# Attention steps in another order, angle tables in pieces, and one step instead of two per panel in the first units

## The reference, cut to what matters

```
scores = jnp.einsum("bcqhd,bckhd->bchqk", qc, k_band).astype(jnp.float32) / math.sqrt(d)
scores = jnp.where(valid, scores + bias[None, None], NEG_INF)
probs = jax.nn.softmax(scores, axis=-1).astype(v.dtype)
out = jnp.einsum("bchqk,bckhd->bcqhd", probs, v_band)            # units 0 to 3
...
w = (p1 - lam * p2).astype(vt.dtype)
return jnp.einsum("bhqk,bhkd->bhqd", w, vt)                      # units 4 to 7
...
ang = positions.astype(jnp.float32)[..., None] * inv_freq
return jnp.cos(ang)[:, :, None, :], jnp.sin(ang)[:, :, None, :]
```

## Time and profile before

| | us |
|---|---|
| median of 3 runs | 1624.08 (1623.08 to 1628.35) |
| the profiled execution | 1629.7 |
| its span, first to last instruction | 1627.8 |
| PE busy | 1523.2 (94%) |
| DVE busy | 845.3 (52%) |
| ACT busy | 617.6 (38%) |
| POOL busy | 179.6 (11%) |

### The profile page before, as it was taken

How to read it: one execution, slowest core, us unless ns; L and a number is a source line. 1 busy time by engine, 2 the same in 40 slices (tenths; PEclk the granted TensorE clock), 3 DMA queues, 4 the chain that set the end, 5 groups by cost and what they waited for, 6 DMA issues and landing times.

```text
span 1627.8 us, 18609 instructions
## 1 busy us (share of the span) xinstructions
PE 1523.2 (94%) x7194; PEld 1207.5 (74%) x7194; DVE 845.3 (52%) x1441; ACT 617.6 (38%) x1117; POOL 179.6 (11%) x121
## 2 busy tenths in 40 slices
PE   7988999999899999999889879998999999999996
PEld 5766667788688888888667669666677788888885
DVE  4544455434753444434656876335445665565454
ACT  4544346422452323323445522215334443343233
POOL 0001100001200000000222251000001121121012
PEclk9999999999899999999898979799999999999998
DMA  6221111232323233323321100001123233233221
GB/s 228 78 72 65 53 54 64 78 91 78 104 78 103 92 102 93 100 95 91 110 91 54 63 1 20 27 27 39 53 98 97 78 104 117 91 101 95 91 76 53
DMA packets 39687, 130.22 MB, mean 80 GB/s; under 512 B 4656, under 2 KB 5040, under 8 KB 39600
## 3 DMA queue, kind: packets, MB, share of 16 engines
q1 hardware_dynamic: 39600, 129.03, 24.9%
HBM read 124.82 MB, written 4.19 MB: 79 GB/s over the span
## 4 chain that ended last, share of the span: by engine, by line
PE 81%; DVE 8%; ACT 6%; issue 3%; POOL 1%; DMA 1%; DVEq 0%; SPq 0%; ACTq 0%; POOLq 0%
PE bank L1022 79%; DVE Fm L1662 3%; ACT Fm L1333 3%; PE bank L1025 2%; ACT Whi L1333 2%; DVE Fm L1654 1%; DVE Fm L1749 1%; DVE Wlo L1654 1%; POOL Fm L2205 1%; ACT L1333 0%; DMA Wraw<-in_w_in_dram 0%; DVE sm L1658 0%; DVE Fm L1658 0%; DMA Fm<-in_relb_dram 0%; DVE sm L1662 0%
## 5 line engine op out<-in xcount | busy, mean ns | idle before, releaser
L1022 PE MATMUL bank<-Rm,Whi 128*128 128x512 f32 x2816 | 885.5, 396 | 0.0
L1022 PEld LDWEIGHTS bank<-Rm,Whi 128*128 128x128 f32 x2816 | 541.0, 192 | 112.5 <-issue 0.8
L1022 PE MATMUL bank<-Rm,Wlo 128*128 128x512 f32 x1408 | 572.1, 406 | 21.8 <-DVE Rm L1654 11.3
L1654 DVE TENSOR_TENSOR Wlo<-Wraw,Whi 128x1024 fp32r<-128x1024 f32 (+1 forms) x211 | 258.7, 1228 | 179.2 <-ACT Whi L1333 178.8
L1022 PEld LDWEIGHTS bank<-Rm,Wlo 128*128 128x128 f32 x1408 | 270.7, 192 | 103.3 <-issue 47.1
L1333 ACT ACTIVATE Whi<-Wraw 128x1024 fp32r<-128x1024 f32 (+1 forms) x224 | 232.6, 1042 | 218.8 <-PE bank L1022 210.6
L2205 POOL TENSOR_TENSOR Fm<-Fm 128x512 f32<-128x512 f32 x94 | 142.8, 1527 | 920.1 <-ACT Fm L1333 371.6
L1022 PE MATMUL bank<-Xr,Whi 128*128 128x512 f32 x736 | 226.6, 389 | 0.0
L1333 ACT ACTIVATE Fm<-bank 128x512 f32<-128x512 f32 (+4 forms) x243 | 102.7, 455 | 234.5 <-PE bank L1022 156.3
L1022 PEld LDWEIGHTS bank<-Xr,Whi 128*128 128x128 f32 x736 | 138.2, 188 | 28.7
L1022 PE MATMUL bank<-Xr,Wlo 128*128 128x512 f32 x368 | 143.2, 389 | 0.0
(11 more groups left out here) (90 smaller groups left out, 806.6 us busy)
## 6 DMA issues: line engine op xcount, KB each, us to landing
Wraw<-in_w_in_dram SPq DMA_DIRECT2D x68, 512.0 KB, 3.5
Wraw<-in_w_ff_dram SPq DMA_DIRECT2D x64, 512.0 KB, 3.5
Wraw<-in_w_up_dram SPq DMA_DIRECT2D x44, 512.0 KB, 3.5
Wraw<-in_w_o_dram SPq DMA_DIRECT2D x16, 512.0 KB, 3.6
Wraw<-in_w_down_dram SPq DMA_DIRECT2D x16, 512.0 KB, 3.5
Wraw<-in_w_ab_dram SPq DMA_DIRECT2D x8, 512.0 KB, 3.5
Wraw<-in_w_down_end_dram SPq DMA_DIRECT2D x8, 384.0 KB, 2.9
Fm<-in_x_dram SPq DMA_DIRECT2D x8, 256.0 KB, 6.1
```

Of the source, the lines that this page charges most:

```text
L1022: return e.matmul(o, l, r, start=first, stop=last)
L1654: return e.tensor_tensor(o, x, y, op)
```

## The change

`heads()` has a new order within a step: `norm` of the last step's scores, `value`, `score`, and `turn` last. `unit_b()` gets the same order with `mix` and `vtok`; its `mix` and `turn` move one step later and its `vtok` too, so that a unit has seven steps before `rmsb` in place of six. `STEPS_A` goes from 2 to 1. The tables' work on DVE is cut in two parts a table (`turns`, `rest`), with a panel between them.

```diff
-STEPS_A, STEPS_B, STEPS_GATE = 2, 2, 2
+STEPS_A, STEPS_B, STEPS_GATE = 1, 2, 2
...
     def heads(u):
         do("obank", u)
         for i in range(7):
-            if 2 <= i <= 5:
-                do("turn", u, 2 * i - 4)
-                do("turn", u, 2 * i - 3)
+            if 1 <= i <= 4:
+                do("norm", u, i - 1)
             if i >= 3:
                 do("value", u, i - 3)
             if i < 4:
                 do("score", u, 2 * i)
                 do("score", u, 2 * i + 1)
-            if 1 <= i <= 4:
-                do("norm", u, i - 1)
+            if 2 <= i <= 5:
+                do("turn", u, 2 * i - 4)
+                do("turn", u, 2 * i - 3)
             yield
...
     def unit_b(u):
-        for i in range(6):
+        for i in range(7):
+            if 1 <= i <= 4:
+                do("mix", u, 2 * i - 1)
+            if i >= 3:
+                do("vtok", u, 2 * i - 5)
             if i < 4:
                 do("score", u, 2 * i)
                 do("score", u, 2 * i + 1)
-                do("mix", u, 2 * i + 1)
-            if 1 <= i <= 4:
-                do("turn", u, 2 * i - 1)
-            if i >= 2:
-                do("vtok", u, 2 * i - 3)
+            if 2 <= i <= 5:
+                do("turn", u, 2 * i - 3)
             yield
...
-        do("cos")
-        yield
-        do("sin")
-        yield
+        for table in ("cos", "sin"):
+            do("turns", table)
+            yield
+            do("rest", table)
+            yield
+            do(table)
...
     for u in range(4):
-        if u > 0:
-            run(tables, 1)
         for j in range(3):
+            if u > 0:
+                run(tables, 1)
             n = first[j] if u == 0 else project("w_in", 4 * j + u, STEPS_A)
             do("plain", n)
```

More of the change, by code:

```diff
@@ L566 @@
     "v_small": {
-        "cos": ("cos_arg",), "sin": ("sin_arg",), "lambda": ("lam_sums",), "subln": ("sub",), "halfgate": ("half",),
+        "rest": ("angle",), "lambda": ("lam_sums",), "subln": ("sub",), "halfgate": ("half",),
         "convw": ("cw",), "baturn": ("baf", "ba"), "wba": ("wba_lo",), ("gates2", 0): ("bet", "absal"),
@@ L1395, in scalar_engine @@
                 elif what == "cos":
-                    w.wait_ge(*sig("cos_arg", "cos"))
+                    w.wait_ge(*sig("angle", "rest", "cos"))
                     act(F(COS), F(COS), ACT.Sin).then_inc(SG["a_small"], 1)
                 elif what == "sin":
-                    w.wait_ge(*sig("sin_arg", "sin"))
+                    w.wait_ge(*sig("angle", "rest", "sin"))
                     act(F(SIN), F(SIN), ACT.Sin).then_inc(SG["a_small"], 1)
@@ L1691, in vector_engine @@
                     own(ts(F(ANG), F(ANG), small("freq"), ALU.mult))
[L1693 to L1697, removed]
+                elif what == "turns":
+                    table, = i
+                    shift, magic = 0.25 if table == "cos" else 0.0, 12582912.0
                     own(ts(F(TURN), F(ANG), 1.0 / (2 * math.pi), ALU.mult, shift, ALU.add))
@@ L1700, in vector_engine @@
                     own(ts(F(TURN), F(TURN), magic, ALU.subtract))
+                elif what == "rest":
+                    table, = i
+                    shift, dst = (0.25, COS) if table == "cos" else (0.0, SIN)
+                    c1, c2 = 6.28125, 0.0019350051879882812
+                    c3 = 2 * math.pi - c1 - c2
                     own(stt(F(dst), F(TURN), -c1, F(ANG), ALU.mult, ALU.add))
```

## The result

| | before | after |
|---|---|---|
| median of 9 runs each, us | 1624.57 (1620.92 to 1628.35) | 1635.26 (1629.80 to 1639.96) |
| the profiled execution, us | 1629.7 | 1639.96 |
| its span, us | 1627.8 | 1638.0 |

The ratio is 1.0066 with an interval of 1.0047 to 1.0084: slower by 10.7 us. The forecast was slower by 29 us, 1653. The sign held, the size did not. Even the low end of the main case's own range, 1638, was missed.

What follows compares the result with a forecast made beforehand. PE, busy 1523.2 us, was taken as the bound, so every term is PE idle time, half clock or stops. First-stretch waits 6.7, gate panel 1.9, stops 1.9, second stretch 10.6, clock 8: +29 on 1624.1, about 1653 us; range 1612 to 1672.

Steps and rivals of the forecast that it cites:

- main case: Whole kernel: longer waits, stops and half clock make it slower, about 1653 us, own range 1638 to 1665; chance 0.54.
- waits, units 0 to 3: First attention stretch: PE waits mostly for late copies, 0.5 us in unit 0, then 3.6, 5.0 and 3.8; 12.9 us.
- waits, units 4 to 7: First attention stretch: `mix` behind the `Wlo` split delays masks and copies, 4.8 us a unit, 19.2 us in all.
- waits of the first stretch against before: Units 0 to 7: waits of 32.1 us against 25.4 before, +6.7 us; bounds -20.0 and +18.7.
- behind the last gate panel: Panel 40 waits while ACT does `feat`'s copy and a table load first: 2.75 us against 0.9, +1.9 us.
- stops: First stretch: nine more places where PE leaves a panel, 0.2 us each, +1.9 us, at most +3.4.
- second stretch, waits: Units 8 to 11: closer steps meet the longer loop, +2.4, +3.6, +3.1 and +1.5, together +10.6 us; bounds -5.5, +16.
- clock: Both attention stretches: seven more waits over 2 us, each followed by 2.3 us lost at half clock, halved to +8 us.
- mechanism of the waits: Attention steps: `value` and `vtok` wait for a copy now last on ACT; 0.7 us with DVE free, more behind other work.
- clock in full: Rival: every new 2 us stall drags 6.8 us at half clock, 24 us in place of 8, 1669 us; chance 0.19.
- Copies in time: Rival: behind 384 and 512-key steps copies land before PE returns, so old waits go; -27 us, 1597 us; chance 0.15.
- The even case: Rival: across the attention steps new waits weigh just what the old did, 1627 us; chance 0.12.

Runs made afterwards that it cites:

- copy-first: The changed kernel with `turn` moved ahead of `value` or `vtok` and `score` in `heads()` and `unit_b()`; 1607.33 us, ratio 0.9894 to the kernel before.
- the first experiment: The changed kernel with the old order of a step (turn, value, score, norm) in units 8 to 11 alone; 1625.34 us, ratio 1.0004 to the kernel before.

## Why the prediction was right or wrong

Its steps in order; "us of half clock" are summed from the stretches that the records show below full speed; each is priced at half of its length. That is a high price: between 345 and 1015 us, in work that is the same in all kernels, 20.5 us more of half clock went with only 7.3 to 7.7 us more of time.

| term | forecast | measured |
|---|---|---|
| waits, units 0 to 3 | 12.9 | 10.45 |
| waits, units 4 to 7 | 19.2 | 14.3 |
| waits of the first stretch against before | +6.7 | -0.7 |
| behind the last gate panel | +1.9 | +2.0 |
| start of the program | none | +1.95 |
| stops | +1.9 | +1.8, as the rest |
| second stretch, waits | +10.6 | +7.9 |
| clock | +8 | -1.7 |
| sum | +29 | +11.3 (span +10.2) |

The 1.1 us too much are in the second stretch, where 7.9 of waits and 3.4 of clock stand against the 10.2 measured.

**The mechanism of the waits was right.** `value` and `vtok` wait for a copy behind `Exp`, and `mix` behind the split prolongs it. Placing `turn` and its copy first took these waits away (copy-first); the split as the blocker was read in the rows at 321.76 to 323.35 and not separately tried. Unit 0 waited 0.76 (said 0.5), unit 1 3.2 (3.6), unit 2 3.9 (5.0), unit 3 2.6 (3.8), unit 9 5.75 (5.7), unit 10 3.35 against 0.54 of before (+2.8, said +3.1), unit 8 +1.8 (+2.4).

**First failed step: the clock, +8 against -1.7, the largest miss.** It said that waits over 2 us would go from three to seven and each would bring 2.3 us, halved. The number of waits was right: seven, 2.44 to 2.87 us. But only two of them were followed by half clock, of 3.4 us each, which is 1.7 us and not 2.3. The sign that the prediction named, a granted clock under 0.97 in the first stretch, came out as 0.99. In after, windows behind waits of 2.44 (at 110.14), 2.45 (150.59), 2.80 (223.75) and 2.79 us (327.72), then behind that of 3.94:

```profile
110.00:115.00 5.00, 4.86 (x23) 3.96 (x24) 1.86 (x3) 2.50 (x5) 0.00 (x0) 0.66 0.01 3
150.00:157.00 7.00, 6.41 (x51) 5.36 (x52) 2.27 (x4) 3.78 (x9) 0.00 (x0) 1.00 0.08 19
223.00:228.00 5.00, 4.25 (x15) 3.74 (x16) 2.40 (x7) 2.71 (x6) 0.00 (x0) 0.66 0.00 0
327.00:334.00 7.00, 6.28 (x36) 5.54 (x37) 3.70 (x10) 3.29 (x7) 0.00 (x0) 1.00 0.10 25
1114.00:1122.00 8.00, 5.77 (x27) 3.27 (x28) 3.38 (x11) 2.42 (x8) 0.00 (x0) 0.79 0.00 0
```

A window of 5 us at 0.66 holds 3.4 us at half clock. And the waits that went had cost more than the new ones: before had 17.0 us of half clock in the first stretch, behind waits of 2.40 (35.71), 4.4, 1.44 (165.81) and 2.06 us (217.15). Three windows of before show those not in the earlier trace rows:

```profile
36.00:40.00 4.00, 4.00 (x12) 2.77 (x11) 1.64 (x9) 3.28 (x10) 0.00 (x0) 0.57 0.00 0
165.00:170.00 5.00, 4.19 (x18) 3.15 (x19) 2.31 (x6) 0.49 (x1) 1.19 (x1) 0.66 0.33 105
217.00:221.00 4.00, 3.85 (x14) 2.92 (x15) 1.43 (x7) 2.54 (x5) 0.00 (x0) 0.57 0.00 0
```

After has 6.8 us there: -5.1 us of time. In the second stretch it rose from 13.6 to 20.4, +3.4, as the forecast had it (+3). The term weighed waits by their length alone and took every one as a coin toss; the gain side was never priced. The -1.7 is of one pair of profiles. With the second profile of after it is 0, and over all profiles with the same order in a stretch half clock was 17.0 in the first stretch before and 6.8 to 10.2 in after, 6.8 to 13.6 in the second with the old order and 17.1 to 20.5 with the new: no pairing reaches more than +3.4 us. So the +8 failed whatever the profile. The prediction also misread its own rows: it counted three of before's seven stretches as short, and five of them are 3.4 us long, which speaks further against the rival of the clock in full.

**Second failed step: the size of the first stretch's waits**, 24.8 against 32.1. In units 4 to 7 both were set somewhat long (2.79 for 3.2; 1.03 for 1.4 + 0.15), 0.9 us a unit, and unit 4 has only the long one, 2.80 in all. In unit 2 the first step with `rope` waited 1.45 us where the chain has 2.75, and unit 3 waited 1.46 + 1.15 in all where it has 3.75. In the second stretch unit 11 came to 5.0 against 5.3 before (said +1.5). Each chain took the latest blocker at its full length; I think it left out that a wait delays PE's next arrival, too, and so shortens the one behind it, but no run isolates that. With the first stretch's waits right and the clock at nothing the sum would have been -0.7 + 1.9 + 1.9 + 10.6 = +13.7.

**The gate panel** was right. ACT's rows in after, which bear out the sum of 0.69, 1.28 and 0.68, and where the load again begins 0.02 us behind the row before it:

```profile
342.17 0.69 ACT L1336 ACTIVATE Xr<-bank,sm 128x512 fp32r<-128x512 f32 x1 [1.56 <-PE bank L1028]
342.88 1.28 ACT L1336 ACT_TABLE_LOAD   x1
...
344.17 0.69 ACT L1336 ACTIVATE Fm<-bank,sm 128x512 f32<-128x512 f32 x1
...
345.00 0.47 PE L1025 MATMUL bank<-Rm,Wlo 128*128 128x512 f32 x1 [2.87 <-ACT Fm L1336]
```

The longer wait of 4.1 us, an estimate by the drain that the Trainium skill ("ScalarE: Activation LUTs", section "What ACT_TABLE_LOAD costs") gives, did not come.

**Stops.** Waits and clock leave 3.8 us of the first stretch unaccounted for. 1.95 of them had arisen before its first transposition, which leaves 1.8, as the forecast's 0.2 a stop gives for nine stops. It is a rest of four terms and not a measurement.

**The rivals.** Copies in time is false for this change (3.8 us of waits in each of units 5 to 7). Its price, -27 us, was for the order as it stood; copy-first made the copies timely by an edit and came to -17 against before. Clock in full is false. The even case was right about the first stretch and wrong about the second.

**What stays open.** The parts don't add up. Alone they give -4.2 (tables), -0.2 (`heads` in units 0 to 3), +6.4 (`unit_b`), with one step a panel -9 on the whole, together -7.0; all of them at once gave +0.8 (the first experiment). In the profiles, from the first transposition, the parts are -4.6, +1.2, +6.2 and -8.3, together -5.5, and all at once -2.0. I think part of the gap is how each edit shifts steps against panels and so where the clock falls, but this was not taken apart. Nor is it known why a wait of 2.44 us was followed by half clock and one of 2.45, 40 us later, was not.

## What to carry to other kernels

In a pipelined attention loop, follow what the next step's first PE instruction needs back through each engine's queue: a copy of 0.4 us behind this step's `Exp` comes the whole way from mask to `Exp`, 3 us, later than the mask, and PE waits for what of this its other work doesn't cover. Putting last step's transposition and copy first gave 28 us here. Price a reordering for each stretch by the time PE is away between steps: the same order was even in units 0 to 3, where four groups of matmuls stood between two steps, and cost 11 us in units 8 to 11, where mostly fewer did (these differ in their other work too). Count the start of a profile apart from the stretch that you edited: here 2 us of it hid a gain. And reckon the clock on both sides, for the waits that go as well as for those that come, with an error as large as the term.

## What the runs showed of the hardware

- **Not every wait costs the clock.** Of the seven waits of 2.4 to 2.9 us in after's first stretch, two were followed by 3.4 us at half clock, and three when the same kernel ran again. In its second stretch it was six of the nine of 1.5 us or more, and six of eight when it ran again. Before, waits of 1.44 and 2.06 us were followed by it too.
- **Half clock varies where nothing changes.** Between the two attention stretches, in work that is the same in all kernels, it summed to 82.0 us in the profiles of before and after and to 61.4 in others. From the landmark at 345 us to the matmul at 1015.3, behind the same sequence of matmuls in every kernel, PE took 670.3 us in the former and 662.6 to 663.1 in the latter, 7 to 8 us of time. One such window, of the kernel with only the tables changed:

```profile
345.00:1040.00 695.00, 653.16 (x3116) 533.64 (x3116) 381.86 (x556) 247.94 (x420) 97.71 (x65) 0.96 0.23 78
```

  The clock there is 0.96 against 0.94 in after. So two single profiles may differ by 8 us of span in code that nobody changed, nearly as much as this change, and stretches must be compared by landmarks and medians.
